# A mixture-of-experts tail in one large kernel: expert rows added to two arrays in turn, already gated, and a last norm that works two tiles apart

## The reference, cut to what matters

```python
scores = sigmoid(h @ router_w)            # 64 experts in 8 groups, 8 chosen for each token
wts = wts / sum(wts) * 2.5                # weights of the 8 chosen experts
# for each block of (token, expert) pairs:
hid = silu(xb @ w1[e]) * (xb @ w3[e])     # 1024 -> 256
acc = acc.at[tok].add(wt[:, None] * (hid @ w2[e]))
shared = (silu(h @ sw1) * (h @ sw3)) @ sw2
f = acc + shared
x = layernorm(DN_ALPHA * x + g2 * f, ln2_w, ln2_b)   # the last operation: the output
```

## Time and profile before

| | us |
|---|---|
| median of 3 timed runs (lowest, highest) | 5107.22 (5101.8, 5116.49) |
| the profiled execution | 5059.33 |
| its span, first to last instruction | 5057.5 |
| route stage, about | 3797.6 to 3963.3 |
| expert stage, first transposes to last matmul | 3971.7 to 4961.6 |
| last norm, first SP issue to the last one's end | 4982.1 to 5057.5 |

### The profile page before, as it was taken

How to read it: one execution, slowest core, us unless ns; L and a number is a source line. 1 busy time by engine, 2 the same in 40 slices (tenths; PEclk the granted TensorE clock), 3 DMA queues, 4 the chain that set the end, 5 groups by cost and what they waited for, 6 DMA issues and landing times. The chain is left out here.

```text
span 5057.5 us, 68248 instructions
## 1 busy us (share of the span) xinstructions
PE 4293.7 (85%) x27634; PEld 2406.0 (48%) x27634; DVE 1984.6 (39%) x4148; ACT 1360.4 (27%) x3110; POOL 520.9 (10%) x564
## 2 busy tenths in 40 slices
PE   6998799999997999999987626787688899999992
PEld 2454466644444665444456515676235343333331
DVE  1631556613515663321026576665345111111115
ACT  2111545511115553111024333332032111111110
POOL 0000000000000000000000001221003322222220
PEclk8999889999998999999988857988798899999996
DMA  4011000120210004311110030000303688889884
GB/s 184 21 62 67 5 14 14 71 84 27 64 65 5 14 14 163 117 51 67 67 61 2 2 97 2 3 3 2 108 0 125 263 259 275 276 296 337 303 262 131
DMA packets 147952, 503.23 MB, mean 100 GB/s; under 512 B 22721, under 2 KB 71474, under 8 KB 134194
## 3 DMA queue, kind: packets, MB, share of 16 engines
q1 hardware_dynamic: 110338, 377.80, 20.0%
q0 software_dynamic: 37296, 120.99, 9.1%
HBM read 402.42 MB, written 96.32 MB: 99 GB/s over the span
## 5 line engine op out<-in xcount | busy, mean ns | idle before, releaser
L697 PE MATMUL banks<-arena 128*128 128x512 f32 (+1 forms) x2928 | 1108.2, 540 | 16.5 <-DMA arena<-in_w_in 10.8
L697 PEld LDWEIGHTS banks<-arena 128*128 128x128 f32 x2928 | 559.0, 191 | 564.0 <-issue 522.8
L3100 PE MATMUL banks<-arena 128*32 128x512 f32 (+2 forms) x2896 | 560.5, 594 | 3.1 <-DMA arena<-in_experts 2.3
L884 PE MATMUL banks<-arena 128*128 128x512 f32 (+1 forms) x896 | 373.5, 571 | 23.4 <-DMA arena<-y_d 17.7
L1248 PE MATMUL banks<-arena 96*128 96x512 f32 (+1 forms) x800 | 376.9, 554 | 11.7 <-ACT arena L1351 10.0
L3100 PEld LDWEIGHTS banks<-arena 128*32 128x32 f32 (+2 forms) x2896 | 197.8, 130 | 356.9 <-issue 354.2
L1298 DVE TENSOR_REDUCE arena<-banks 128x1 f32<-128x512 f32 (+1 forms) x400 | 238.1, 595 | 242.6 <-PE banks L1248 241.1
L3120 PE MATMUL banks<-arena 128*32 128x512 f32 (+2 forms) x1448 | 296.3, 615 | 1.3 <-ACT arena L3178 1.3
L884 PEld LDWEIGHTS banks<-arena 128*128 128x128 f32 x896 | 171.6, 193 | 218.6 <-issue 213.3
L3067 POOL DMA_INDIRECT r_d<-arena x125 | 181.4, 1451 | 702.5 <-DMA r_d<-arena 278.3
L3157 DVE SCALAR_TENSOR_TENSOR arena<-arena,banks 128x256 f32<-128x256 f32 x79 | 38.1, 482 | 533.9 <-ACT arena L3192 533.9
(11 more groups left out here) (507 smaller groups left out, 5658.4 us busy)
## 6 DMA issues: line engine op xcount, KB each, us to landing
arena<-in_experts SPq DMA_DIRECT2D x64, 3072.0 KB, 12.9
arena<-in_ada_w SPq DMA_DIRECT2D x12, 2048.0 KB, 7.6
arena<-in_w_in SPq DMA_DIRECT2D x19, 1024.0 KB, 5.7
arena<-in_w_mod SPq DMA_DIRECT2D x8, 2048.0 KB, 17.9
arena<-in_w_in SPq DMA_DIRECT2D x7, 2048.0 KB, 8.9
arena<-in_w_out SPq DMA_DIRECT2D x6, 2048.0 KB, 10.6
arena<-in_w_mod SPq DMA_DIRECT2D x8, 1024.0 KB, 5.2
u<-arena POOLq DMA_DIRECT2D x28, 256.0 KB, 2.3
```

The costliest lines, as they stand in the source:

```text
L697: i = e.matmul(self.out_of(n), lhs, rhs, start=k == 0, stop=k == KT - 1)
L884: i = e.matmul(bank(n % 4)[:, 0:nn], w[:, q, :], H[:, q, t0:t0 + nn], start=q == 0, stop=q == KT - 1)
L3100: op = e.matmul(ABK[(q - q0) % 2][rows, :], xT[(q - q0) % 2][:, P * k:P * k + P][:, rows], weights[:, i % SLOTS, 512 * k:512 * k + 512], s ...
```

## The change

**Adds to two arrays.** `xa_d` goes, a second array `r1_d` comes. Rows of experts with an even number are added to the first array, of those with an odd number to the second, so the first piece of expert i waits for the pieces of expert i-2. The second array is filled with zeros by one DMA of 6 MB on SP's queue in the route stage (the first is written by the shared expert's stores).

**Gated already.** `g2r` is made at the start of the route stage, by one product on DVE, two matmuls of 512 columns and one copy. What goes into the arrays has been multiplied by it. In the expert stage DVE alone takes the down product out of PSUM, multiplying by `g2r`; ACT has no part in it. In the shared expert DVE multiplies the down product by `g2r` and adds the residual tokens from SBUF, where before ACT copied and SP stored them apart; the tile is then stored once. These steps of DVE are laid between the eight `slots_of`.

**Last norm.** The two arrays' tiles are added, the multiplication by g2 is gone, and ACT does the subtraction and scaling (as scale and bias of one activation). DVE does the statistics of tile i, the scale of tile i-1 and the weight and bias of tile i-2 in one turn.

```diff
-                  "h_d": [NX + 4 * P, D], "xa_d": [NX, D], "r_d": [NX + 4 * P, D], "l_d": [P * 256, 2]}
+                  "h_d": [NX + 4 * P, D], "r_d": [NX + 4 * P, D], "r1_d": [NX + 4 * P, D], "l_d": [P * 256, 2]}
...
         def route_sync(e):
...
+            e.wait_ge(*Vn.at("zero"))
+            ld.turn(e)
+            e.dma_start(r_d[1].rearrange("(a p) n -> p a n", p=P), zt.unsqueeze(1).broadcast_to([P, NR // P, D])).then_inc(ld.hit("route", "zr1"), 16)
             for q in range(9):
...
                 if q:
-                    e.wait_ge(*SC.of("shared").at("out", q - 1))
+                    e.wait_ge(*VC.of("shared").at("sum", q - 1))
                     ld.turn(e)
-                    e.dma_start(r_d[P * (q - 1):P * q, :], sog[(q - 1) % 2]).then_inc(ld.hit("shared", "r", q - 1), 16)
+                    e.dma_start(r_d[0][P * (q - 1):P * q, :], sog[(q - 1) % 2]).then_inc(ld.hit("shared", "r", q - 1), 16)
...
         def route_tensor(e):
+            e.wait_ge(*Vn.at("diag"))
+            for n in range(2):
+                op = e.matmul(both[:, 512 * n:512 * n + 512], ones, dg[:, 512 * n:512 * n + 512], start=True, stop=True)
+            op.then_inc(Tn.hit("spread"), 1)
             e.wait_ge(*ld.at("route", "w"))
...
             for ti in range(2, 8):
                 slots_of(ti)
-                if ti in (2, 5):
-                    next(shared)
+                next(shared, None)
             steps(shared)
...
+        def shared_vector(e):
+            Tn, Vn, Sn, Gn = points("shared")
+            for q in range(9):
+                if q < 8:
+                    e.wait_ge(*Sn.at("silu", q))
+                    if q >= 2:
+                        e.wait_ge(*Tn.at("turn", q - 2))
+                    e.tensor_tensor(shd[q % 2], ssg[q % 2], ABK2[q % 2][:, 256:512], ALU.mult).then_inc(Vn.hit("hid", q), 1)
+                if q:
+                    p = q - 1
                     e.wait_ge(*Tn.at("down", p))
                     if p >= 2:
                         e.wait_ge(*ld.at("shared", "r", p - 2))
-                    e.activation(sog[p % 2], OBK, ACT.Copy).then_inc(Sn.hit("out", p), 1)
+                    e.wait_ge(*Vn.own())
+                    e.tensor_tensor(sog[p % 2], OBK, g2r, ALU.mult).then_inc(Vn.hit("out", p), 1)
+                    e.wait_ge(*Sn.at("turned", turn_at["X", p]))
+                    e.wait_ge(*Vn.own())
+                    e.tensor_tensor(sog[p % 2], sog[p % 2], xst[p % 2], ALU.add).then_inc(Vn.hit("sum", p), 1)
                 yield
...
                 def scatter(q):
                     e.wait_ge(*Vn.at("out", q))
-                    e.wait_ge(*Sn.at("out", q))
                     for n, (i, rows) in enumerate(self.rows[q]):
-                        if i and self.of[i][0] == (q, n):
-                            for before in self.of[i - 1]:
+                        if i >= 2 and self.of[i][0] == (q, n):
+                            for before in self.of[i - 2]:
                                 e.wait_ge(*st.at(S, "r", *before))
                         st.turn(e)
-                        e.indirect_dma_start(r_d, ...
+                        e.indirect_dma_start(r_d[i % 2], ...
...
-                    e.tensor_copy(og[(q - q0) % 3][:, 0:512], OBK[:, 0:512]).then_inc(Vn.hit("out", q), 1)
+                    e.tensor_tensor(og[(q - q0) % 3], OBK, g2r, ALU.mult).then_inc(Vn.hit("out", q), 1)
...
-                    e.activation(og[(q - q0) % 3][:, 512:1024], OBK[:, 512:1024], ACT.Copy).then_inc(Sn.hit("out", q), 1)
...
         def end_sync(e):
+            def rows(i):
+                if i >= 3:
+                    e.wait_ge(*Vn.at("done", i - 3))
+                for n, half in enumerate((rr, r1)):
+                    ld.turn(e)
+                    e.dma_start(half[i % 3], r_d[n][P * i:P * i + P, :]).then_inc(ld.hit("end", "r", n, i), 16)
+
+            rows(0), rows(1)
             row_bcast(e, w2r, A["ln2_w_2"][0], "end", "w")
             row_bcast(e, b2r, A["ln2_b_2"][0], "end", "b")
-            for i in range(8):
-                if i >= 3:
-                    e.wait_ge(*Vn.at("normed", i - 3))
-                ld.turn(e)
-                e.dma_start(rr[i % 3], r_d[P * i:P * i + P, :]).then_inc(ld.hit("end", "r", i), 16)
-                ld.turn(e)
-                e.dma_start(xr[i % 3], xa_d[P * i:P * i + P, :]).then_inc(ld.hit("end", "x", i), 16)
-                if i >= 2:
-                    store(i - 2)
+            rows(2)
+            for i in range(8):
                 e.wait_ge(*Vn.at("done", i))
                 ld.turn(e)
                 e.dma_start(out[0][P * i:P * i + P, :], rs[i % 3]).then_inc(ld.hit("end", "out", i), 16)
+                if i + 3 < 8:
+                    rows(i + 3)
...
+            for i in range(10):
+                if i < 8:
+                    stats(i)
+                if 1 <= i < 9:
+                    scale(i - 1)
+                if i >= 2:
+                    last(i - 2)
...
+                if i:
+                    p = i - 1
+                    e.wait_ge(*Vn.at("scale", p))
+                    if p >= 3:
+                        e.wait_ge(*ld.at("end", "out", p - 3))
+                    e.activation(rs[p % 3], rr[p % 3], ACT.Identity, bias=nb[:, p:p + 1], scale=sd[:, p:p + 1]).then_inc(Sn.hit("normed", p), 1)
```

More of the change, by code:

```diff
@@ L2656, in moe_sparse @@
         diu = di.bitcast(U32)
[L2657 removed]
+        dg = al(1024)
         both = ps[:, 512:1536]
@@ L2665, in moe_sparse @@
         sog = [sh(1024), sh(1024)]
-        stg = [sh(1024) for _ in range(4)]
+        stg, xst = [sh(1024), sh(1024)], [sh(1024), sh(1024)]
         ABK2, HBK, OBK = [bank(3), bank(7)], bank(4), ps[:, 2560:3584]
@@ L2673, in route_sync @@
         def route_sync(e):
+            Tn, Vn, Sn, Gn = points("route")
             ld.turn(e)
@@ L2729, in route_tensor @@
             steps(shared)
-            e.wait_ge(*SC.of("shared").at("turned", len(turns) - 1))
-            for n in range(KT):
-                e.wait_ge(*Vn.at("diag", n))
-                op = e.matmul(both[:, P * n:P * n + P], ones, dg, start=True, stop=True)
-                op.then_inc(Tn.hit("spread", n), 1)
         def route_scalar(e):
@@ L2752, in route_vector @@
                 e.tensor_copy(inv[:, i:NB:4, 0].bitcast(U32), s1[:, 2:3].broadcast_to([P, len(range(i, NB, 4))])).then_inc(Vn.hit("blank"), 1)
-            e.memset(zt, 0.0).then_inc(Vn.hit("zero"), 1)
             e.memset(word, 0.0).then_inc(Vn.hit(), 1)
+            e.wait_ge(*Tn.at("spread"))
+            e.tensor_copy(g2r, both).then_inc(Vn.hit("row"), 1)
             for i in range(4):
@@ L2927, in turn_rows @@
                     e.wait_ge(*Sn.at("turned", n - 1))
+                else:
+                    e.wait_ge(*VC.of("route").at("row"))
                 for k in range(KT):
@@ L2955, in shared_tensor @@
                     if p:
-                        e.wait_ge(*Sn.at("out", p - 1))
+                        e.wait_ge(*Vn.at("out", p - 1))
                     for n in range(2):
@@ L2968, in rows_out @@
                 e.wait_ge(*Tn.at("turned", n))
-                if n >= 4:
-                    e.wait_ge(*ld.at("route", "h", n - 4))
-                e.activation(stg[n % 4], both, ACT.Copy, scale=1.0 if kind == "H" else ALPHA).then_inc(Sn.hit("turned", n), 1)
+                if ti >= 2 and kind == "H":
+                    e.wait_ge(*ld.at("route", "h", ti - 2))
+                elif ti >= 2:
+                    e.wait_ge(*Vn.at("sum", ti - 2))
+                e.activation((stg if kind == "H" else xst)[ti % 2], both, ACT.Copy, scale=1.0 if kind == "H" else ALPHA).then_inc(Sn.hit("turned", n), 1)
             for q in range(9):
@@ L3114, in down @@
                         e.wait_ge(*Vn.at("out", q - 1))
-                        e.wait_ge(*Sn.at("out", q - 1))
                     for n in range(2):
@@ L3178, in turn_h @@
                     e.activation(hT[(q - q0) % 2], HBK[:, 0:256], ACT.Copy).then_inc(Sn.hit("hT", q), 1)
-                def down(q):
-                    e.wait_ge(*Tn.at("down", q))
-                    if q >= q0 + 3:
-                        for n in range(len(self.rows[q - 3])):
-                            e.wait_ge(*st.at(S, "r", q - 3, n))
-                    e.activation(og[(q - q0) % 3][:, 512:1024], OBK[:, 512:1024], ACT.Copy).then_inc(Sn.hit("out", q), 1)
                 turn_x(q0)
@@ L3299, in end_vector, with last @@
-                e.wait_ge(*Vn.own())
-                e.tensor_tensor(o_, o_, b2r, ALU.add).then_inc(Vn.hit("done", i), 1)
+                e.scalar_tensor_tensor(nb[:, i:i + 1], mv[:, 2 * i:2 * i + 1], -1.0, sd[:, i:i + 1], ALU.mult, ALU.mult).then_inc(Vn.hit("scale", i), 1)
+            def last(i):
+                if i == 0:
+                    e.wait_ge(*ld.at("end", "w"))
+                    e.wait_ge(*ld.at("end", "b"))
+                e.wait_ge(*Sn.at("normed", i))
```

(3 more changed lines are left out.)

79 lines of the change are left out of this document (27 added, 52 removed).

## The result

The changed kernel takes 5029.2 us (median of 4 runs, 5028.3 to 5045.7), the kernel before 5106.7 in the same comparison (4 runs): ratio 0.9854, interval 0.9835 to 0.9873, so 65 to 84 us faster. I had predicted 5065 us with a range of 5042 to 5094. The direction was right, the time lies 13 us under the range.

A forecast was written before the change was run, and what follows sets the result against it. PE was taken to bound the expert stage except at late gathers, POOL the route stage, DVE the last norm. Terms -53.7 - 1.9 + 1.0 + 12.5 = -42.1, set against the median 5107.2, gave 5065 us, range 5042 to 5094.

The forecast's parts named there:

- Expert stage, -53.7: Expert stage: two arrays remove PE's waits for late gathers and their low clock, 61.4 x 7/8; bounds -61.4 and -20.
- the eighth that I kept: Expert stage: one of the eight gather waits assumed to remain because DMA landings might get longer.
- Last add, -1.9: End of expert stage: the last add no longer waits 5.35 us for another expert's landing; bounds -2.4 and 0.
- the first loads of the norm, -1.3: Last norm: first pair of loads goes ahead of weight and bias, -1.3 us, counted inside the +12.5.
- Route stage, +1.0: Route stage: making g2r at the start delays the scores by up to 1.7 us, partly regained; bounds 0 to 2.
- cover of 8 us for the last slots: Route stage: slots of tile 7 ready at 3938, wanted by POOL at 3946.3, so DVE's added work costs 0.
- Last norm, +12.5: Last norm: five DVE waits of 6.4 us for loads behind `done`, stage 79.2 against 65.4; bounds -19 and +20.
- estimate of 3.2: Last norm: landing time in us for half a megabyte by the Trainium skill's fit; the trace's 5.5 was preferred.
- the first (DMA as the bound): Expert stage, late part: DMA becomes the bound, waits and low clock there stay, -26 us, 5081 us; chance 15%.
- rival 4: Expert stage: adds and gathers in flight together stretch landings, deciding at 31 us; slower, 5124 us; chance 6%.
- Rival 2: Expert stage: the two arrays do less, half of the stalls stay, -19 us, 5088 us; chance 9%.
- rival 3: Last norm: loads come faster, 4 us of wait instead of 6.4, -12 more, 5053 us; chance 10%.

The follow-up runs named there:

- fifth run: The changed kernel unaltered, timed again on chip 7: 5009.2 us against 5066.1 for the kernel before, ratio 0.9892.
- norm8: Changed kernel with eight buffers for each of the two arrays in the last norm, no load waiting for `done`: 4983.5 us, ratio 0.9859.
- before_paced: Kernel before, with list writes of tile t (from tile 3) waiting for ACT's last shared-expert output of tile t-1: 5070.4 us, ratio 0.9951.
- lists_paced: Changed kernel with eight norm buffers, three tiles loaded before weight and bias; list writes of tile t (from 3) wait for sum t-1: 4990.0 us, ratio 0.9794.
- before_two: Kernel before with only the two arrays in turn, zeros and a third load and sum in the norm: 5008.3 us, ratio 0.9899.
- one_no_zeros: Changed kernel with one array for all adds, no zeros written, the norm reading that array twice: 5082.4 us, ratio 1.0047.
- lists_last: Changed kernel with eight norm buffers, three tiles loaded before weight and bias; all list writes held until the shared expert's last sum: 5047.8 us.
- after: The changed kernel itself in its first profile and comparison, chip not known: 5029.2 us, ratio 0.9854.
- before_third: Kernel before, unaltered, profiled a third time, on chip 11: 5104.7 us, beside 5110.1 for the kernel before on the same chip.
- before: The unchanged kernel in its first profile, chip not known: 5107.2 us timed, 5059.3 us in the profiled execution.
- before_again: Kernel before, unaltered, profiled once more, on chip 5: 5062.9 us, beside 5058.5 for the kernel before on the same chip.

## Why the prediction was wrong, point by point

**Expert stage, -53.7.** Right in its mechanism, small by the eighth that I kept: all waits went, and the stage is 930.1 us instead of 989.3, -59.2. The price of a wait with its low clock (61.4 / 44.6 = 1.38 us) is within the 1.3 to 1.4 that five profiles show. The executions differ in their stalls, so that the same change is worth 51 to 71 us (981.1 and 1001.1 less 930).

**Last add, -1.9, and the first loads of the norm, -1.3.** From PE's last product to DVE's first instruction of the norm it is 28.3 us before and 24.1 after (24.7 in the fifth run): -3.6 to -4.2 for -3.2.

**Route stage, +1.0.** On the chips without late signals +1.9 (165.7 to 167.6), inside the bounds of 0 and 2. The zeros cost nothing, as taken. The cover of 8 us for the last slots was there: in the fifth run they are ready at 3940.0 us and POOL comes to them at 3950.7. On the chips with late signals the term fails, in its sign too: -20 us (210.9 to 191.1, both on chip 11). In the first profile after, the slots of tile 5 keep POOL for 17.4 us and those of tile 7, ready at 3962.2 instead of 3938, for 2.2, and yet the stage is shorter than that of the kernel before on such a chip.

**Last norm, +12.5.** With the 1.3 us that I had put in this term it was 79.2 us for the stage: measured 79.5, five waits of 6.34 to 6.55. The loads behind them land 4.5 to 5.6 us after their issue, so the 5.5 from the trace of before was the number to take, not the estimate of 3.2. norm8 shows that the waits go with the wait for `done`.

**The step that failed** is the last: "the change is a matter of waits that both have, so I set it against the median", and with it the route term of +1.0. The sum of -42.1 us was made from the trace of an execution without late signals, and there it stands: stage by stage it is -46.2 between that trace and the fifth run's (start +1.8, route +1.9, first gather to PE -1.1, expert -59.3, gap -3.6, norm +14.1), by the timed runs on chip 7 -55 (-42 to -68). The timed executions of 5107 us have no trace; that they hold 45 us more in the route stage is read from chip 11, where the kernel before takes 5110 us. The change takes 20 of those away. With -20 for +1.0, and -59.2 for -53.7 in the expert stage, the sum would be -68.6 us (5039 us), inside the measured 65 to 84 us faster; but both numbers are known only from the runs.

The reason lies in a side effect that I had counted as harmless. DVE now has the shared expert's products and sums between its slot tiles. When PE's signals are late, DVE is late with the slots, POOL stops writing lists for 17.4 us, and the lateness ends at 23 to 25 us; in the kernel before POOL writes on to the end and it grows to 40. That such a pause has this effect is shown by before_paced and lists_paced; that it comes from DVE's order of work is read from the traces, and no run has this order alone on a chip with late signals.

I had the sign of this in hand: 48 us between a profile and its median are more than all but one term of my sum. The rivals all were of the expert stage and the norm; none asked where those 48 us lie. That the direction came out right owes nothing to this: it was right on both kinds of chip by the expert stage.

Of the rivals, the first (DMA as the bound) falls: share 0.96 and PE busy throughout. The Trainium skill's rule that I weighed against the change (DMA: Bandwidth & Descriptors, section Issuing engines are not separate DMA queues) is that DMAs started by any engine run on the same 16 engines and interleave. What I drew from it came half true: the adds did get slower, and it did not matter. Their landings (min, median, max us) with two arrays (fifth run; before_two on chip 5 has the same three numbers), then with one (one_no_zeros, chip 5):

```profile
DMA to landing us min/median/max: 6.0/11.2/16.1
```

```profile
DMA to landing us min/median/max: 3.5/8.8/16.6
```

11.2 us is still below the two blocks, 23 us, that an array now has. Gathers get slower too, with a median of 10.9 us for 9.1, but their maximum stays at 23.4, so rival 4, which needed 31, falls. Rival 2 falls with the stalls gone, rival 3 by the waits of 6.4.

## What to carry to other kernels

Where adds into one array must follow one another, a second array takes the landing out of the loop for the price of one more load and sum at the end. A buffer given back by the last reader's end, with the next load behind it, costs a whole landing per turn: count the buffers against the order of the instructions, not against their number. And before a sum is set against a median, ask where the difference between the profile and the median lies: if it is larger than the terms of the sum, the change may work on it too.

## What the runs showed of the hardware

PE's signals can arrive late, on some chips and not on others. On chips 0, 10, 11 and 12 every profile with list writes beside PE's work has signals 8 to 40 us late; on chips 5 and 7 none of five is over 0.1 us in the middle of the writes. POOL issues a list write of 128 rows of 8 bytes every 1.28 us; the first signal that is late is of PE work that ended when 13 or 14 of them were out. The lateness grows while they go on and ends when they stop: in the seven such profiles without added pauses the latest signal arrives 2.2 to 6.1 us after the end of the write before the pause, or of the last one (0.1 to 2.9 us after a write in the three with added pauses, where it is 8 to 11 us late). Without writes beside PE's work there is none (lists_last). In the same stretch ACT's signals to PE are on time: PE starts 0.05 to 0.06 us after ACT's end in `after` and before_third.

The records of semaphores thin out in that stretch as well. From 3880 to 3940 us the traces of the kernels without added pauses hold 967 to 1061 updates on chips 5 and 7 (`before` too, 1056), and 157 to 201 where signals are late; the source line of the list writes (L2914) has landings in before_again and none in before_third. So whether landings were late there cannot be told. Nor can it be told whether the recording has a share in the lateness: every execution here comes with a recorded span and clock, and none was timed without. Why PE's signals, and what about these writes (their number, their size or their own signals), was not separated. Gathers and adds in the expert stage, two or three in 12 us, do no such thing: 929 to 930 us on all six chips.
